# Experts: where one-hot rows and first splits stand in the order, how FFN weights are issued, and how the last expert's product is laid out

## What is computed

```python
def swiglu(h, w_gate, w_up, w_down):
    return (jax.nn.silu(h @ w_gate) * (h @ w_up)) @ w_down

def moe_swiglu(h, router, w_gate, w_up, w_down):
    t = h.reshape(-1, d)
    logits = (t @ router).astype(jnp.float32)
    top_v, top_i = lax.top_k(logits, TOP_K)          # 2 of 8
    top_w = jax.nn.softmax(top_v, axis=-1)
    gates = jnp.sum(jax.nn.one_hot(top_i, N_EXPERTS) * top_w[..., None], axis=1)
    for e in range(N_EXPERTS):                       # d_ff of an expert: 3584
        y_e = swiglu(t, w_gate[e], w_up[e], w_down[e])
        out = out + gates[:, e:e + 1] * y_e
```

## Time and profile before

| | before |
|---|---|
| median of 3 runs | 2800.96 us |
| the profiled execution | 2800.72 us |
| its span | 2798.8 us |
| TensorE matmul busy | 2560.9 us, 92% |
| VectorE busy | 1713.6 us, 61% |
| ScalarE busy | 1264.7 us, 45% |
| mean granted TensorE clock | 0.954 |
| moved by DMA | 593.6 MB, 212 GB/s |

### The profile page before, as it was taken

One profiled execution on the slowest core, in us unless ns is written; L12 is line 12 of the kernel. 1 busy time (PEld: TensorE's weight loads), 2 busy tenths in 40 slices (PEclk: granted clock), 3 DMA queues, 4 the chain that ended last, 5 costly groups with the idle time before them and its releaser, 6 DMA issues.

```text
span 2798.8 us, 36295 instructions
## 1 busy us (share of the span) xinstructions
PE 2560.9 (92%) x13970; PEld 2185.2 (78%) x13970; DVE 1713.6 (61%) x1592; ACT 1264.7 (45%) x1100; POOL 68.6 (2%) x37
## 2 busy tenths in 40 slices
PE   8699997677999999999999998899789999996999
PEld 6499884664787877878787877898569989974898
DVE  4445444443788887878787887454735455545455
ACT  2433301212676766767676766333033343311333
POOL 0000001111000000000000000000100000001000
PEclk9899998887999999999999999999899999998999
DMA  8265140004899999989898997653416575522453
GB/s 313 91 200 180 60 150 31 1 1 143 289 358 331 348 339 329 353 317 369 310 368 312 358 330 277 222 180 105 150 32 203 190 244 181 193 77 75 156 189 128
DMA packets 313023, 593.59 MB, mean 212 GB/s; under 512 B 8704, under 2 KB 132736, under 8 KB 312704
## 3 DMA queue, kind: packets, MB, share of 16 engines
q1 hardware_dynamic: 312960, 592.70, 60.2%
HBM read 591.62 MB, written 1.05 MB: 212 GB/s over the span
## 4 chain that ended last, share of the span: by engine, by line
PE 70%; DVE 5%; ACT 2%; DVEq 1%; DMA 1%; issue 1%; SPq 0%; PEldq 0%; POOL 0%; ACTq 0%; PEld 0%
PE bank L182 20%; PE bank L183 20%; PE bank L184 20%; PE bank L453 3%; PE bank L1916 2%; DVE scratch L2055 2%; PE bank L1559 1%; DVEq L2056 1%; PE bank L1582 1%; DVE weights_lo L1762 1%; ACT weights_hi L1663 1%; DMA scratch<-in_ffn_w_gate 1%; PE bank L1125 0%; PE bank L1124 0%; PE bank L1116 0%
## 5 line engine op out<-in xcount | busy, mean ns | idle before, releaser
L1762 DVE TENSOR_TENSOR weights_lo<-mslot,weights_hi 128x2048 fp32r<-128x2048 f32 x336 | 770.8, 2303 | 184.0 <-ACT weights_hi L1663 183.0
L1663 ACT ACTIVATE weights_hi<-mslot 128x2048 fp32r<-128x2048 f32 x336 | 642.1, 1918 | 251.2 <-PE bank L184 240.6
L601 DVE TENSOR_TENSOR weights_lo<-scratch,weights_hi 128x2048 fp32r<-128x2048 f32 x165 | 376.9, 2292 | 377.5 <-ACT weights_hi L594 374.9
L182 PE MATMUL bank<-x_hi,weights_hi 128*128 128x256 f32 x1760 | 504.0, 286 | 16.1 <-DVE weights_lo L601 9.6
L183 PE MATMUL bank<-x_lo,weights_hi 128*128 128x256 f32 x1760 | 503.3, 286 | 0.0
L184 PE MATMUL bank<-x_hi,weights_lo 128*128 128x256 f32 x1760 | 503.0, 286 | 0.0
L594 ACT ACTIVATE weights_hi<-scratch 128x2048 fp32r<-128x2048 f32 x165 | 315.2, 1919 | 322.4 <-PE bank L184 266.9
L182 PE MATMUL bank<-weights_hi,x_hi 128*128 128x512 f32 x936 | 376.6, 402 | 38.9 <-DVE weights_lo L1762 37.8
L183 PE MATMUL bank<-weights_lo,x_hi 128*128 128x512 f32 x936 | 370.4, 396 | 0.0
L184 PE MATMUL bank<-weights_hi,x_lo 128*128 128x512 f32 x936 | 370.0, 395 | 0.0
L182 PEld LDWEIGHTS bank<-x_hi,weights_hi 128*128 128x128 f32 x1760 | 343.3, 195 | 19.3 <-DVE weights_lo L601 13.7
(11 more groups left out here) (347 smaller groups left out, 2278.2 us busy)
## 6 DMA issues: line engine op xcount, KB each, us to landing
mslot<-in_o_moe_w_gate SPq DMA_DIRECT2D x112, 1024.0 KB, 5.9
mslot<-in_o_moe_w_up SPq DMA_DIRECT2D x112, 1024.0 KB, 5.9
mslot<-in_o_moe_w_down SPq DMA_DIRECT2D x112, 1024.0 KB, 6.1
scratch<-in_ffn_w_gate SPq DMA_DIRECT2D x44, 1024.0 KB, 7.2
scratch<-in_ffn_w_up SPq DMA_DIRECT2D x44, 1024.0 KB, 5.6
scratch<-in_ffn_w_down SPq DMA_DIRECT2D x44, 1024.0 KB, 5.1
mslot<-in_o_w_in SPq DMA_DIRECT2D x8, 2048.0 KB, 7.9
mslot<-in_w_in SPq DMA_DIRECT2D x10, 1536.0 KB, 7.9
```

The costliest lines, as they stand in the source:

```text
L182: pe.matmul(out, stationary[0], moving[0], start=start, stop=False)
L601: dve.tensor_tensor(m.wlo[to][:, :], m.fslot[i], m.whi[to][:, :], ALU.subtract).then_inc(m.sig["f_lo"], 1)
L1663: act.activation(m.whi[(place + half) % PLACES][:, :], r.slot[slot + half], ACT.Copy).then_inc(s["r_hi"], 1)
L1762: dve.tensor_tensor(m.wlo[i][:, :], r.slot[slot + half], m.whi[i][:, :], ALU.subtract).then_inc(s["r_lo"], 1)
```

## The change

Four things are changed.

- `moe_pe`: the drain that raises `r_used` to 3 stands in front of the router. ScalarE splits gate 0's first half before it waits for xn, makes xn_hi, and splits the second half behind it. VectorE's first low split, which stood between the selection and the ranks, comes behind the one-hot rows together with the second.
- `moe_act`, `middle`: the copy of the transposed one-hot rows stands in chunk 2, behind the splits of gate 2 and up 2.
- The last expert (TensorE): the second half of down 5 stands behind the transposes of chunk 6. hidden_hi and hidden_lo of chunk 6 have places of their own (in the gathered tokens' memory); ScalarE makes hidden_hi between the two halves of down 6's split. The last down product runs by output half: all of the first 512 columns, then all of the second. y is split, brought back and added by output half.
- `ffn_load`: the order is gate 0, up 0, gate 1, down 0, up 1, then for each further unit gate(u + 1), down(u), up(u + 1); the four mixer blocks stand one each between down(u) and up(u + 1) of units 1 to 4.

```diff
-def ffn_load(sp, m, v, w_gate, w_up, w_down, between):
+def ffn_load(sp, m, v, w_gate, w_up, w_down, ahead):
...
-    gate_up(0)
+    gate(0)
+    up_(0)
+    gate(1)
     down(0)
-    between()
-    gate_up(1)
-    down(1)
-    with sp.Fori(2, NU) as u:
-        gate_up(u)
+    up_(1)
+    for u, block in enumerate(ahead, 1):
+        gate(u + 1)
         down(u)
+        load_block(sp, m, block)
+        up_(u + 1)
+    with sp.Fori(1 + len(ahead), NU - 1) as u:
+        gate(u + 1)
+        down(u)
+        up_(u + 1)
+    down(NU - 1)
...
+    r.hh_last, r.hl_last = r.xgh[:, 0:FC // P, :], r.xgl[:, 0:FC // P, :]
...
 def moe_pe(pe, m):
     s, r, c = m.sig, moe_mem(m), m.c
+    pe.drain().then_inc(s["r_used"], PE_AHEAD)
...
-
-    pe.drain().then_inc(s["r_used"], PE_AHEAD)
...
-        with pe.Fori(2, NC) as ch:
+        if gather_next:
...
+            return
+        with pe.Fori(2, NC - 1) as ch:
             chunk(q, ch)
+        pe.wait_ge(s["r_silu"], q * NC + NC - 1)
+        inner(q, 0, "gate", NC - 1)
+        turn(q * NC + NC - 2)
+        inner(q, 1, "up", NC - 1)
+        down(q, NC - 2, parts=(0,))
         pe.wait_ge(s["r_silu"], q * NC + NC)
         turn(q * NC + NC - 1)
-        if gather_next:
-            pe.wait_ge(s["r_ohT"], q + 1)
-            gather(q + 1)
-        down(q, NC - 1, final=True)
+        down(q, NC - 2, parts=(1,))
+
+    def last_down(q):
+
+        pe.wait_ge(s["r_hl"], q * NC + NC)
+        for side in range(2):
+            cols = slice(side * HALF, (side + 1) * HALF)
+            for half, (hi, lo) in halves(q, "down", NC - 1, FC // P // 2):
+                for j in range(FC // P // 2):
+                    k = half * FC // P // 2 + j
+                    last = split_product(pe, m.ps[3 + side][:, :], (r.hh_last[:, k, :], r.hl_last[:, k, :]),
+                                         (hi[:, j, cols], lo[:, j, cols]), start=False, stop=k == FC // P - 1)
+            last.then_inc(s["r_side"], 1)
...
-    def chunk(q, c):
+    def chunk(q, c, copy_rows=False):
         hi(q, "gate", c)
         hi(q, "up", c)
+        if copy_rows:
+            act.wait_ge(s["r_ohTp"], q + 1)
+            act.activation(r.ohT, m.ps[7][:, 0:SEQ], ACT.Copy).then_inc(s["r_ohT"], 1)
         hi(q, "down", c - 1, halves=(0,))
...
     def middle(q):
         chunk(q, 1)
-        act.wait_ge(s["r_ohTp"], q + 1)
-        act.activation(r.ohT, m.ps[7][:, 0:SEQ], ACT.Copy).then_inc(s["r_ohT"], 1)
-        with act.Fori(2, NC) as c:
+        chunk(q, 2, copy_rows=True)
+        with act.Fori(3, NC) as c:
             chunk(q, c)
...
-    hi(0, "gate", 0)
+    hi(0, "gate", 0, halves=(0,))
     act.wait_ge(s["r_xn"], 1)
     act.activation(r.xnh, m.xn, ACT.Copy).then_inc(s["r_xnh"], 1)
+    hi(0, "gate", 0, halves=(1,))
...
     middle(final)
+    hi(final, "down", NC - 1, halves=(0,))
+    hidden_hi(final * NC + NC - 1, r.hh_last)
+    hi(final, "down", NC - 1, halves=(1,))
     act.wait_ge(s["r_used"], moe_used(final, "down", NC - 2))
     ffn_hi(act, m, 1, "gate", 0)
-    y_hi(final)
+    y_hi(final, last=True)
...
+            lo(q, "down", NC - 1, halves=(0,))
+            hidden_lo(q * NC + NC - 1, r.hh_last, r.hl_last)
+            lo(q, "down", NC - 1, halves=(1,))
...
-    lo(0, "gate", 0, halves=(0,))
     dve.wait_ge(s["r_rank"], 1)
...
-    lo(0, "gate", 0, halves=(1,))
+    lo(0, "gate", 0)
```

More of the change, by code:

```diff
@@ L1561, in gather, with halves @@
             last.then_inc(s["r_gath"], 1)
-    def halves(q, kind, ch, k):
+    def halves(q, kind, ch, k, parts=(0, 1)):
         number, place, _, _ = moe_piece(kind, ch)
-        for half in range(2):
+        for half in parts:
             pe.wait_ge(s["r_lo"], q * PIECES + number + half + 1)
@@ L1583, in turn, with down @@
         last.then_inc(s["r_hT"], 1)
-    def down(q, ch, first=False, final=False):
+    def down(q, ch, first=False, final=False, parts=(0, 1)):
         pe.wait_ge(s["r_hl"], q * NC + ch + 1)
-        for half, (hi, lo) in halves(q, "down", ch, FC // P // 2):
+        for half, (hi, lo) in halves(q, "down", ch, FC // P // 2, parts):
             for j in range(FC // P // 2):
@@ L1625, in middle, with last_back @@
         last.then_inc(s["r_ohTp"], 1)
-        with pe.Fori(2, NC) as ch:
-            chunk(q, ch)
+        if gather_next:
+            with pe.Fori(2, NC) as ch:
+                chunk(q, ch)
+            pe.wait_ge(s["r_silu"], q * NC + NC)
+            turn(q * NC + NC - 1)
+            pe.wait_ge(s["r_ohT"], q + 1)
+            gather(q + 1)
+            down(q, NC - 1, final=True)
+            return
+        with pe.Fori(2, NC - 1) as ch:
+            chunk(q, ch)
+        pe.wait_ge(s["r_silu"], q * NC + NC - 1)
[3 more added lines that the diff above has]
+        down(q, NC - 2, parts=(0,))
         pe.wait_ge(s["r_silu"], q * NC + NC)
         turn(q * NC + NC - 1)
-        if gather_next:
-            pe.wait_ge(s["r_ohT"], q + 1)
-            gather(q + 1)
-        down(q, NC - 1, final=True)
+        down(q, NC - 2, parts=(1,))
[9 more added lines that the diff above has]
+            last.then_inc(s["r_side"], 1)
+    def last_back(q):
+        for half in range(2):
+            pe.wait_ge(s["r_yl"], 2 * q + half + 1)
+            cols = slice(half * HALF, (half + 1) * HALF)
+            for t in range(NT):
+                bank = m.ps[((5, 6), (7, 2))[t][half]]
+                pe.matmul(bank[:, :], r.ohT[:, t * P:(t + 1) * P], r.yh[:, cols], start=True, stop=False)
+                pe.matmul(bank[:, :], r.ohT[:, t * P:(t + 1) * P], r.yl[:, cols], start=False,
+                          stop=True).then_inc(s["r_scat"], 1)
     pe.wait_ge(s["r_xnh"], 1)
@@ L1687, in chunk, with y_hi @@
         hi(q, "down", c - 1, halves=(1,))
-    def y_hi(q):
-        act.wait_ge(s["r_used"], moe_used(q, "down", NC - 1))
+    def y_hi(q, last=False):
+        if not last:
+            act.wait_ge(s["r_used"], moe_used(q, "down", NC - 1))
         for side in range(2):
+            if last:
+                act.wait_ge(s["r_side"], side + 1)
             act.activation(r.yh[:, side * HALF:(side + 1) * HALF], m.ps[3 + side][:, :],
@@ L1715, in moe_act @@
         middle(q)
+        hi(q, "down", NC - 1)
+        hidden_hi(q * NC + NC - 1)
         hi(q + 1, "gate", 0, halves=(0,))
@@ L1809, in middle @@
         hidden(q, NC - 1)
-        lo(q, "down", NC - 1)
-        hidden_lo(q * NC + NC - 1)
+        if more:
+            lo(q, "down", NC - 1)
+            hidden_lo(q * NC + NC - 1)
+        else:
+            lo(q, "down", NC - 1, halves=(0,))
+            hidden_lo(q * NC + NC - 1, r.hh_last, r.hl_last)
+            lo(q, "down", NC - 1, halves=(1,))
     first_best(r.lg, r.m1, r.sel1)
@@ L1866, in moe_dve @@
     y_lo(final)
[L1867 to L1870, removed]
+    add(final, 0, 0, last=True)
+    add(final, 1, 0, last=True)
+    add(final, 0, 1, last=True).then_inc(s["n_res"], 2)
+    add(final, 1, 1, last=True).then_inc(s["n_res"], 1)
     norm_scale(dve, m, AFTER_EXPERTS, 0)
@@ L2146, in _ @@
                 load_block(sp, m, i)
[L2148 to L2151, removed]
+            ffn_load(sp, m, 0, w["e_ffn_w_gate"][0], w["e_ffn_w_up"][0], w["e_ffn_w_down"][0],
+                     range(B_ODD, B_ODD + 4))
             for i in range(B_ODD + 4, B_SECOND):
@@ L2156, in _ @@
                 first = B_SECOND + 8 * l
[L2158 to L2161, removed]
+                ffn_load(sp, m, 1 + 2 * l, w["ffn1_w_gate_2"][l], w["ffn1_w_up_2"][l], w["ffn1_w_down_2"][l],
+                         range(first, first + 4))
                 for i in range(first + 4, first + 8):
```

24 lines of the change are left out of this document (12 added, 12 removed).

## The result

The changed kernel takes 2724.86 us (median of 4 runs, 2723.89 to 2725.79) against 2801.18 us for the kernel before in the same rounds: a ratio of 0.973, 95% interval [0.9716, 0.9743], 76.3 us less. The forecast was 2728 us with a range of 2718 to 2742. The profiled execution took 2724.61 us, its span is 2722.7 us.

The account below looks back on a forecast made before the run. TensorE, busy 92% of the span, was taken as the bound, so time could fall only at its waits or low clock. 53.3 + 4.6 + 3.3 + 11.4 = 72.6 us off 2800.7 gave 2728 us, range 2718 to 2742.

Parts of the forecast that it names:

- Step 1: Expert loop, all eight experts: moving the one-hot copy removes TensorE's stall, 6.66 us an expert, -53.3 us.
- rival C: Experts' weight slots: without the stalls' rest, transfers become the bound and time grows, 2811 us; chance 0.02.
- Step 2: Start of the experts: earlier splits bring the gather forward, with VectorE's selection held by POOL's xn_lo; -4.6 us.
- rival A: Start of the experts: the port doesn't hold small operations, so the gain is 9.0 us, 2724 us; chance 0.12.
- Step 3: Last expert: reordered down 5, transposes, splits and last product by output half bring the norm earlier; -3.3 us.
- part 3: The last expert's new order, forecast at -3.3 us.
- Step 4: FFN behind the experts: gate 1 issued ahead of the mixer blocks removes TensorE's 9.6 us wait; -11.4 us.
- part 2: The new start of the experts, before the first gather, forecast at -4.6 us.

Follow-up runs that it names:

- e1: Kernel before with only the copy of the one-hot rows moved behind the splits of gate 2 and up 2; 2745.71 us, ratio 0.9805.
- e6: Changed kernel with four of the six expert weight slots in use (a piece waits for piece n - 4); 2725.76 us.
- e7: Changed kernel with three expert weight slots in use (a piece waits for piece n - 3); 2827.1 us.
- e9: Changed kernel with a wait added: POOL starts xn_lo only when VectorE's selection is over; 2722.36 us, ratio 0.9723.
- e4: Kernel before with only the last expert's new order; 2793.90 us, ratio 0.9974.
- e3: Kernel before with only the new start: drain ahead of the router, xn_hi behind one split, VectorE's first low split behind the one-hot rows; 2797.14 us, ratio 0.9989.
- the one with both edits: Changed kernel with xn_lo made on VectorE and up 0's splits behind the norm after the experts; 2718.44 us, run again 2717.94 us.

## Why the prediction was right, and where it was off

**Step 1, the copy.** Right in cause and nearly in size: 6.54 us an expert on the mean (52.3 / 8), where 6.66 was forecast. The two one-hot transposes that stay cost 0.28 us (17.05 - 16.77), and I had given them 0.2; and the last three stalls had cost 6.75 to 6.8 us rather than 6.86. The margin of 1.1 us was real, and no queue behind the copy came late. e1 shows the gain comes from this edit alone.

**The transfers (rival C).** Charging nothing was right. The forecast rate was 358 GB/s; it is 359, and e6 and e7 put the limit between three slots and four. The DMA share of 0.99 in that window looks like a full queue, yet two slots could be taken away for 1.5 us.

**Step 2, the start.** The choice between 4.6 us (held) and 9.0 us (rival A) was the one real fork, and the hold decided it: 4.7 us. That rested on one row about a large operation, a split of 2.29 us that took 6.33; the changed kernel's 4.48 us row now shows it for an operation of 16 columns. The Trainium skill (SBUF — State Buffer, Who interferes with whom) states that the loser blocks for the whole instruction; the trace agrees for both sizes. It also lists tensor_scalar among the operations that can take the shared pair with one input, in a mode that their operands must allow, and the 2.12 us row of e9 agrees. What I had left out is the 1.0 us behind the gather: gate 0 to the first transposes took 18.17 us in place of 19.14, with the same matmuls and no wait in either. Over the first 6 us from gate 0's start the granted clock was 0.73 on the mean, 0.56 before. It was named in the range only. It belongs to this part: over all fourteen profiles the stage took 19.14 to 19.16 us in the four kernels with the old start, 18.14 to 18.19 in the six profiles with the new one, 18.50 to 18.55 in the three with xn_lo on VectorE, and 19.30 in e9. Why the low stretch ends where it does in each of them, no run shows.

**Step 3, the last expert.** 3.3 us as forecast (the rows of that step give 16.4 - 12.95 = 3.45, written as 3.3), and so in its inner numbers: the last product ended 12.4 us after up 6 (forecast 12.3), the wait in it was 0.69 us (0.8), and the clock didn't fall at it:
```profile
1669.10 0.50 PE L182 MATMUL bank<-weights_hi,x_hi 128*128 128x512 f32 x1 [0.69 <-DVE weights_lo L1814]
1669.44 0.40 PE L183 MATMUL bank<-weights_lo,x_hi 128*128 128x512 f32 x1
```
But 1.8 us of the forecast were the low clock behind the old wait (7.3 - 5.5), and e1 has that wait without the low clock: 1.6 of the 3.3 us come there without part 3, and 1.2 us are lost behind norm 4. So half of this term hangs on where a low stretch falls, which the forecast took as given, and that it came out exact is partly luck.

**Step 4, the loads.** 11.3 for 11.4 us. Nothing came late in the four units with a block.

**What the sum missed.** The terms measure 52.3 + 4.7 + 3.3 + 11.3 = 71.6 us against 72.6. The changed kernel is nevertheless 3 us faster than forecast, since three stages outside the sum came out shorter, 4.4 us together: the 1.0 us behind the gather, which is part 2's, 1.1 us before norm 3, and 2.3 us in the mixer behind the second FFN. The stage before norm 3 took 645.9 to 648.5 us over all profiles, 646.85 and 647.77 in two of the same changed kernel, so 1.1 us there is no effect of the change that these profiles can tell. The mixer was shorter in e1 and e4 as well, which have the old loads, so the new order of the loads isn't its cause. Windows at the start of that mixer, before and after, in this order:
```profile
1948.00:1954.00 6.00, 4.98 (x18) 3.99 (x19) 2.96 (x8) 3.75 (x7) 0.00 (x0) 0.72 0.01 3
```
```profile
1874.00:1880.00 6.00, 4.70 (x25) 4.08 (x26) 2.95 (x8) 3.96 (x8) 0.00 (x0) 1.00 0.00 0
```
The same gap in the norm is followed by a stretch at the low level in one and not in the other; why, these runs don't show. My sum had no term for any of it; what it had wrong is the 0 that it put for all other stages: they gave 4.4 us here, inside the range. Without the 3.4 us that no edit explains, the changed kernel would stand at 2728.3 us, on the forecast, since part 2's extra 1.0 us makes up for the 1.0 us that the four terms fell short. That, too, is luck.

## What to carry to other kernels

A wait in an engine's queue costs what stands behind it, not what it protects: 0.38 us of copying cost 6.5 us an expert, because the next split was queued behind its wait. Move such a step to where its condition has been met anyway, and check the slack of the work that it passes. Before moving work onto an idle engine or beside other work, ask which of the two holds the other: here POOL's 4.5 us beside a chain of small VectorE operations kept the gather back by 4.2 us (3.8 up to the first transposes), and a wait *added* to POOL brought it forward by 2.4 (1.3). And an order of loads is read by the piece that is needed first, not by the slot that is free first.

## What was not expected

- **Stages without an edit differ by up to 3.5 us between kernels.** Norm 1 to silu 0 of the first FFN took 27.05 us before and 25.31 after, with the same instructions; over all fourteen profiles it is 25.3 to 25.4, 25.9 or 27.0 to 27.2 us, with a granted clock of 0.93 on the mean in the shorter ones and 0.87 in the longest. Norm 5 to norm 6 took 122.7 or 122.8 us in the kernel before and in e3, and 119.3 to 120.9 us in all the others. Norm 6 to the end took 732.8 to 735.2 us, at an equal mean clock (0.968). Part of this differs between two profiles of the same kernel: the one with both edits had 27.19 us and then 25.87 in the first of these stages, 119.56 and 120.94 in the second. Part of it came again: the changed kernel's two profiles agree within 0.15 us in all three. A gain of 2 us read from two whole runs can be that alone. What sets the value in a given kernel, I did not settle.
- **A short operation is held as long as a long one.** 0.17 us became 4.48 us, and 2.29 us became 6.33, some 4 us more in both; a duration far above an operation's usual one, ending with POOL's, is the sign to look for.
- **The queues' share.** A DMA share of 0.98 to 1.02 and 359 to 373 GB/s stood here beside two slots that were hardly needed, and with three slots, where the loads were the bound, the share was lower (0.92). The share alone said nothing about whether loads were the bound.
